# An encoder layer with 32 experts on one core: transposes moved to VectorE, expert matrices loaded in 16 KB runs

## The reference

```python
u2 = modulate(rmsnorm(x, norm_ffn_g[l]), sh_ffn, sc_ffn)     # h * (1 + scale) + shift
# route: sigmoid(u2 @ w_router), best of 8 groups, then top 2 of its 4 experts
def expert_block(args):
    xblk, e = args
    h = jax.nn.silu(xblk @ w_gate[e]) * (xblk @ w_up[e])       # 1024 -> 512
    return h @ w_down[e]                                       # 512 -> 1024
x = x + gt_ffn * (sum over a token's two experts of weight * expert output)
return rmsnorm(x, final_g)
```

## Time and profile before

| | |
|---|---|
| median of three runs | 1627.49 us (1622.82 to 1628.82) |
| the profiled execution | 1622.71 us, its span 1620.9 us |
| mean granted TensorE clock | 0.962 of full speed |
| busy share of the span | PE 92%, PEld 65%, DVE 50%, ACT 27%, POOL 33% |
| DMA | 345.05 MB in 167551 packets, mean 213 GB/s |
| chain that ended last | PE 77%, DMA 11%, DVE 7%, rest 5% |

### The profile page before, as it was taken

The page is one execution under the profiler, slowest core; times in us unless marked ns, Lnnn a source line. Parts: engine busy times, 40 slices in busy tenths (PEclk is TensorE's granted clock), DMA queues, the critical chain, the costliest instruction groups (busy, mean ns, idle before and its releaser), DMA issues.

```text
span 1620.9 us, 32501 instructions
## 1 busy us (share of the span) xinstructions
PE 1486.0 (92%) x12727; PEld 1052.6 (65%) x12727; DVE 815.1 (50%) x1192; ACT 437.4 (27%) x812; POOL 534.7 (33%) x458
## 2 busy tenths in 40 slices
PE   4899999999999999999998998499699798989994
PEld 3677787777778887787886886355355454545551
DVE  4655544555673324445223744455365544645556
ACT  5455553344461112002002321111111111111113
POOL 2532224333344323323231110244243333424453
PEclk9899999999999999999999998699899999989998
DMA  9570113222214333342121612999999999999997
GB/s 340 150 241 29 31 31 96 69 76 66 62 34 143 115 111 91 118 161 75 49 91 38 213 78 108 405 405 403 408 403 404 403 407 405 403 406 359 402 405 283
DMA packets 167551, 345.05 MB, mean 213 GB/s; under 512 B 28073, under 2 KB 96353, under 8 KB 159281
## 3 DMA queue, kind: packets, MB, share of 16 engines
q1 hardware_dynamic: 138544, 288.72, 47.7%
q0 software_dynamic: 19680, 37.65, 6.7%
q10 hardware_dynamic: 9248, 17.58, 3.5%
HBM read 311.41 MB, written 32.39 MB: 212 GB/s over the span
## 4 chain that ended last, share of the span: by engine, by line
PE 77%; DMA 11%; DVE 7%; ACT 2%; issue 2%; SPq 1%; POOL 1%; ACTq 0%; DVEq 0%; POOLq 0%
PE ps L822 30%; PE ps L1094 15%; DMA w_exp<-in_w_exp_up 8%; PE ps L991 7%; PE ps L1104 7%; PE ps L1015 4%; PE ps L886 2%; PE ps L859 2%; PE ps L1077 2%; PE ps L912 1%; PE ps L950 1%; PE ps L961 1%; PE ps L1084 1%; PE ps L873 1%; DVE br_lo L1608 1%
## 5 line engine op out<-in xcount | busy, mean ns | idle before, releaser
L1094 PE MATMUL ps<-w_exp,xT 128*32 128x256 f32 x4992 | 295.3, 390 | 40.5 <-DMA w_exp<-in_w_exp_up 34.6
L822 PE MATMUL ps<-u_hi,w_hi 128*128 128x512 f32 x768 | 308.5, 402 | 6.8 <-DVE u_lo L1513 6.6
L822 PE MATMUL ps<-u_hi,w_lo 128*128 128x512 f32 x768 | 300.3, 391 | 0.0
L822 PE MATMUL ps<-u_lo,w_hi 128*128 128x512 f32 x768 | 300.0, 391 | 0.0
L1094 PEld LDWEIGHTS ps<-w_exp,xT 128*32 128x32 f32 x4992 | 158.0, 112 | 146.4 <-issue 51.3
L614 POOL CAST w_hi<-w_raw 128x1024 fp32r<-128x1024 f32 x48 | 62.5, 1301 | 382.9 <-PE ps L822 232.7
L1852 DVE COPY w_down<-w_exp 128x4096 f32<-128x4096 f32 x78 | 179.7, 2304 | 0.0
L822 PEld LDWEIGHTS ps<-u_hi,w_hi 128*128 128x128 f32 x768 | 144.9, 189 | 45.3 <-issue 9.7
L822 PEld LDWEIGHTS ps<-u_hi,w_lo 128*128 128x128 f32 x768 | 144.7, 188 | 31.1
L822 PEld LDWEIGHTS ps<-u_lo,w_hi 128*128 128x128 f32 x768 | 145.1, 189 | 29.3 <-issue 1.0
L1104 PE MATMUL ps<-w_down,actT 128*32 128x256 f32 x2496 | 150.9, 382 | 2.7 <-DVE w_down L1852 2.7
(11 more groups left out here) (282 smaller groups left out, 2131.3 us busy)
## 6 DMA issues: line engine op xcount, KB each, us to landing
w_exp<-in_w_exp_gate SPq DMA_DIRECT2D x32, 2048.0 KB, 26.6
w_exp<-in_w_exp_up SPq DMA_DIRECT2D x32, 2048.0 KB, 29.3
w_exp<-in_w_exp_down SPq DMA_DIRECT2D x32, 2048.0 KB, 28.7
ada_g<-in_ada_w ACTq DMA_DIRECT2D x32, 512.0 KB, 3.7
w_raw<-in_w_in SPq DMA_DIRECT2D x24, 512.0 KB, 4.1
w_raw<-in_w_branch_gate SPq DMA_DIRECT2D x24, 512.0 KB, 4.0
d_y<-yb POOLq DMA_DIRECT2D x78, 128.0 KB, 8.6
bias<-d_table SPq DMA_DIRECT2D x48, 192.0 KB
```

What stands on the lines that cost most here:

```text
L822: ins = pe.matmul(ps[:, 5 + h, :], a[par][:, kc, :], b[:, kc, HF[h]], start=(n == 1), stop=(n == MM))
L1094: last = pe.matmul(ps[CAP * n:CAP * (n + 1), 2, 0:QT], x, w[n // 2][:, off:off + QT], start=(kc == 0), stop=(kc == KC - 1))
```

## The change

The transposes inside the expert stage go from TensorE to VectorE, whose `transpose` turns each 32x32 block of a tile in its place. Four things follow from it.

- **Rows.** `row_features` turns `xg_s` straight to `xT`, without PSUM; it waits for the copied rows (`xg_s_ready`) and for the end of the `gate_up` that still reads `xT` (`gu_ps`). `next_rows` of ScalarE waits for `xT_ready` in place of TensorE's transposes. `rows_to_features` and the PSUM bank are gone.
- **Hidden values.** `hidden` multiplies in two halves of 64x128 into a new tile `act_q` of 128x128, which `hidden_features` turns to `actT`. `hidden_to_features` is gone. `gate_up` of the next block waits until both halves are done (`act_ready`), as they read its PSUM bank. VectorE's order becomes `row_features` of p+1, `hidden`, `output_of_last_block`, `hidden_features`, `down_weights`.
- **Orders.** A block-wise turn leaves the features of a token in another order than a whole transpose. So the features of u2 are written in a new order ("place" order): VectorE reads x1, `sc_row`, `sh_row` and `sh_b` with a step of eight floats where it makes u2 and the shift row; `normed_features` then transposes contiguous slices. `gate_up` reads the matrices' columns (its moving operand) with a step of four floats, 16 bytes, where it read runs of 256; the router's rows are laid out to match: SyncE loads them with eight DMAs of 128-byte pieces into `wr_rows`, and GpSimd regroups them by three copies that stand behind its `m_lo` of the second tile and wait for `ld_wr`.
- **Runs.** As the order of features is free now, each partition takes one run of 16 KB of each expert matrix.

The core of the diff:

```diff
@@ -202,15 +202,17 @@
 wr = at("wr", 202, [P, KC, NE])
+wr_rows = at("wr_rows", 203, [P, KC, NE])
...
 xg = [at(f"xg{h}", 192 + h, [P, QT]) for h in range(2)]
-xT = at("xT", 194, [P, 2, P])
+xT = at("xT", 194, [P, KC * CAP])
 xg_s = at("xg_s", 195, [P, QT])
...
 y_s = at("y_s", 197, [P, QT])
-actT = at("actT", 198, [P, 2, 2 * CAP])
+actT = at("actT", 198, [P, FC * CAP])
+act_q = at("act_q", 198.5, [P, FC * CAP])
 yb = [at(f"yb{h}", 199 + h, [P, QT]) for h in range(2)]
@@ -362,10 +364,12 @@
 wo_v = w_out[0].rearrange("(c p) n -> p c n", p=P)
-wr_v = w_router.rearrange("(p c) n -> p c n", c=KC)
-exp_v = {"g": w_exp_gate[0].rearrange("e (q p c) n -> e p q (c n)", q=4, p=P),
-         "u": w_exp_up[0].rearrange("e (q p c) n -> e p q (c n)", q=4, p=P),
-         "d": w_exp_down[0].rearrange("e (h p c) n -> e p h (c n)", h=2, p=P)}
+wr_v = w_router.rearrange("(q f h j) n -> h j f q n", q=4, h=2, j=FC)
+exp_v = {"g": w_exp_gate[0].rearrange("e (p c) n -> e p (c n)", p=P),
+         "u": w_exp_up[0].rearrange("e (p c) n -> e p (c n)", p=P),
+         "d": w_exp_down[0].rearrange("e (p c) n -> e p (c n)", p=P)}
+by_place = lambda a: a.rearrange("p (q j f) -> p q j f", q=4, j=KC)
+by_feature = lambda a: a.rearrange("p (q f j) -> p q j f", q=4, j=KC)
 u2_rows = d_u2.rearrange("t (q n) -> (t q) n", q=4)
@@ -534,13 +538,13 @@
                 sp.dma_start(dst[:], src.partition_broadcast(P)).then_inc(ld_rows, 16)
-    wr_g, wr_vg = wr[:].rearrange("p c (g e) -> p c g e", e=EPG), wr_v.rearrange("p c (g e) -> p c g e", e=EPG)
-    for g in range(NG):
-        sp.dma_start(wr_g[:, :, g, :], wr_vg[:, :, group_at(g), :]).then_inc(ld_wr, 16)
+    for h in range(2):
+        for j in range(FC):
+            sp.dma_start(wr_rows[CAP * j:CAP * (j + 1), h::2, :], wr_v[h, j]).then_inc(ld_wr, 16)
     def load_expert(i, w):
         r, _ = matrix_at(i, w)
-        sp.dma_start(w_exp[r][:].rearrange("p (q n) -> p q n", q=2 if w == "d" else 4), exp_v[w][expert_at(i)]).then_inc(ld_wt[r], 16)
+        sp.dma_start(w_exp[r][:], exp_v[w][expert_at(i)]).then_inc(ld_wt[r], 16)
@@ -702,6 +706,12 @@
         pool.tensor_tensor(m_lo[t % 2][:], merged[:, :, t * P:(t + 1) * P], m_hi[t % 2][:].bitcast(f32), SUB).then_inc(m_ready, 1)
+        if t == 1:
+            pool.wait_ge(ld_wr, 16 * 2 * FC)
+            by_group = lambda a: a.rearrange("p c (g e) -> p c g e", e=EPG)
+            for a in range(3):
+                own = slice(3 * a, min(3 * a + 3, NG))
+                pool.tensor_copy(by_group(wr[:])[:, :, own, :], by_group(wr_rows[:])[:, :, a::3, :]).then_inc(wr_ready, 1)
@@ -772,7 +782,7 @@
 def _(pe):
-    for s_, n_ in ((pr_ps, PR_PRIME), (acc_ps, 1), (gu_ps, 1), (y_ps, 1), (y_evac, 2), (yb_ready, 4), (wd_ready, 1), (actT_ready, 1), (xg_s_ready, 1)):
+    for s_, n_ in ((pr_ps, PR_PRIME), (acc_ps, 1), (gu_ps, 1), (y_ps, 1), (y_evac, 2), (yb_ready, 4), (wd_ready, 1), (actT_ready, 1), (xg_s_ready, 1), (act_ready, 2)):
         pe.sem_inc(s_, n_)
     def mod_vector(v):
@@ -1019,7 +1029,7 @@
         if t == 0:
-            pe.wait_ge(ld_wr, 16 * NG)
+            pe.wait_ge(wr_ready, 3)
         for kc in range(KC):
@@ -1027,9 +1037,8 @@
     def normed_features(t):
         pe.wait_ge(u2_ready, t + 1)
-        v = u2[:, t, :].rearrange("p (q c) -> p c q", c=KC)
         for kc in range(KC):
-            last = pe.transpose(ps[:, 4 + kc // 4, (kc % 4) * P:(kc % 4 + 1) * P], v[:, kc, :], ident[:])
+            last = pe.transpose(ps[:, 4 + kc // 4, (kc % 4) * P:(kc % 4 + 1) * P], u2[:, t, kc * P:(kc + 1) * P], ident[:])
         last.then_inc(x2t_ps, 1)
@@ -1070,46 +1079,30 @@
-    def rows_to_features():
-        v = xg_s[:].rearrange("p (m c) -> p c m", c=2)
-        for c in range(2):
-            last = pe.transpose(ps[:, 0, c * P:(c + 1) * P], v[:, c, :], ident[:])
-        last.then_inc(xg_ps, 1)
-    def hidden_to_features():
-        v = act[2 * CAP:P, :].rearrange("p (m c) -> p c m", c=2)
-        for c in range(2):
-            last = pe.transpose(ps[:, 4, c * 2 * CAP:(c + 1) * 2 * CAP], v[:, c, :], ident[2 * CAP:P, 2 * CAP:P])
-        last.then_inc(ht_ps, 1)
     def gate_up(i):
...
         for kc in range(KC):
-            x = xT[:, kc % 2, CAP * (kc // 2):CAP * (kc // 2 + 1)]
             for n in range(4):
-                off = kc * FE + QT * (n % 2)
-                last = pe.matmul(ps[CAP * n:CAP * (n + 1), 2, 0:QT], x, w[n // 2][:, off:off + QT],
-                                 start=(kc == 0), stop=(kc == KC - 1))
+                cols = w[n // 2][:, kc * FE:(kc + 1) * FE].rearrange("p (c a f j) -> p a c j f", c=2, a=2, j=FC)
+                last = pe.matmul(ps[CAP * n:CAP * (n + 1), 2, 0:QT].rearrange("p (c j f) -> p c j f", c=2, j=FC),
+                                 xT[:, CAP * kc:CAP * (kc + 1)], cols[:, n % 2], start=(kc == 0), stop=(kc == KC - 1))
         last.then_inc(gu_ps, 1)
     def down():
         for fc in range(FC):
-            a = actT[:, fc % 2, CAP * (fc // 2):CAP * (fc // 2 + 1)]
+            a = actT[:, CAP * fc:CAP * (fc + 1)]
             for n in range(4):
...
-    def gate_up_and_next_rows(i, p):
+    def gate_up_of_block(i, p):
         pe.wait_ge(xT_ready, p)
+        pe.wait_ge(act_ready, p * 2)
+        hold(pe)
         gate_up(i)
-        pe.wait_ge(xg_s_ready, p + 2)
-        hold(pe)
-        rows_to_features()
     def down_of_last_block(p):
@@ -1117,26 +1110,17 @@
-    def hidden_rows(p):
-        pe.wait_ge(act_ready, p)
-        hold(pe)
-        hidden_to_features()
     read_ends(12)
-    pe.wait_ge(xg_s_ready, 2)
-    rows_to_features()
     for i in range(NE):
...
         if i == 0:
-            gate_up_and_next_rows(0, 1)
-            hidden_rows(1)
+            gate_up_of_block(0, 1)
         read_ends(1)
         with pe.Fori(ends[i - 1] if i else 2, ends[i]) as p:
-            gate_up_and_next_rows(i, p)
+            gate_up_of_block(i, p)
             down_of_last_block(p)
-            hidden_rows(p)
     down_of_last_block(ends[NE - 1])
@@ -1394,7 +1378,7 @@
         if free is not None:
-            sc.wait_ge(xg_ps, free)
+            sc.wait_ge(xT_ready, free)
         hold(sc)
@@ -1680,9 +1664,11 @@
     dve.wait_ge(ld_rows, 16 * 5)
-    ch.mark(dve.tensor_tensor(sh_row[:], sh_row[:], sh_b[:], ADD))
     ch(dve.tensor_tensor(sc_row[:], sc_row[:], sc_b[:], ADD))
     ch(dve.scalar_tensor_tensor(sc_row[:], sc_row[:], 1.0, g_row[:], ADD, MUL))
+    sh_turned = g_row
+    ch(dve.tensor_tensor(by_place(sh_turned[:]), by_feature(sh_row[:]), by_feature(sh_b[:]), ADD))
     def mix_half(t, h):
@@ -1694,7 +1680,7 @@
         ch(dve.reciprocal(ms2[:, m:m + 1], rstd2[:, m:m + 1]))
-        dve.scalar_tensor_tensor(u2[:, m, :], u2[:, m, :], ms2[:, m:m + 1], sh_row[:], MUL, ADD).then_inc(u2_ready, 1)
+        dve.scalar_tensor_tensor(u2[:, m, :], u2[:, m, :], ms2[:, m:m + 1], sh_turned[:], MUL, ADD).then_inc(u2_ready, 1)
     def lower_features(m):
@@ -1709,7 +1695,7 @@
             lower_features(t - 1)
-        ch(dve.tensor_tensor(u2[:, t, :], x1[:, t, :], sc_row[:], MUL))
+        ch(dve.tensor_tensor(by_place(u2[:, t, :]), by_feature(x1[:, t, :]), by_feature(sc_row[:]), MUL))
     normed(TT - 1)
@@ -1827,12 +1813,20 @@
     def row_features(p):
-        dve.wait_ge(xg_ps, p)
-        dve.tensor_copy(xT[:].rearrange("p a b -> p (a b)"), ps[:, 0, 0:2 * P]).then_inc(xT_ready, 1)
+        dve.wait_ge(xg_s_ready, p + 1)
+        dve.wait_ge(gu_ps, p)
+        hold(dve)
+        dve.transpose(xT[:], xg_s[:]).then_inc(xT_ready, 1)
     def hidden(p):
         dve.wait_ge(silu_ready, p)
-        dve.tensor_tensor(act[2 * CAP:P, :], act[2 * CAP:P, :], ps[2 * CAP:P, 2, 0:QT], MUL).then_inc(act_ready, 1)
+        dve.wait_ge(actT_ready, p)
+        hold(dve)
+        for c in range(2):
+            cols = slice(P * c, P * (c + 1))
+            dve.tensor_tensor(act_q[2 * CAP * c:2 * CAP * (c + 1), :], act[2 * CAP:P, cols], ps[2 * CAP:P, 2, cols], MUL).then_inc(act_ready, 1)
     def output_of_last_block(p):
@@ -1842,8 +1836,11 @@
     def hidden_features(p):
-        dve.wait_ge(ht_ps, p)
-        dve.tensor_copy(actT[:].rearrange("p a b -> p (a b)"), ps[:, 4, 0:4 * CAP]).then_inc(actT_ready, 1)
+        dve.wait_ge(act_ready, p * 2 + 2)
+        dve.wait_ge(y_ps, p)
+        hold(dve)
+        dve.transpose(actT[:], act_q[:]).then_inc(actT_ready, 1)
     def down_weights(i):
@@ -1853,16 +1850,16 @@
     row_features(1)
+    row_features(2)
     hidden(1)
-    row_features(2)
     hidden_features(1)
...
         with dve.Fori(last, end) as p:
+            row_features(p + 1)
             hidden(p)
-            row_features(p + 1)
             output_of_last_block(p)
```

More of the change, by code:

```diff
@@ L336, in build @@
         ld_gmix = sem("ld_gmix")
-        ld_rows, ld_wr = sem("ld_rows"), sem("ld_wr")
+        ld_rows, ld_wr, wr_ready = sem("ld_rows"), sem("ld_wr"), sem("wr_ready")
         mo_ps, x1_half, root2, u2_ready, x2t_ps, u2T_ready, ro_ps = (sem(n) for n in (
@@ L347, in build @@
```

(4 more changed lines are left out.)

## The result

The changed kernel takes 1794.88 us in the median of four runs (1792.34 to 1795.47); the kernel before takes 1625.55 beside it. The ratio is 1.104, with a 95% interval from 1.101 to 1.107: 169 us more, where 12 less were forecast. The profiled execution took 1795.18 us with a span of 1793.2.

A forecast was written before the change was run, and what follows sets the result against it. TensorE's matmuls, broken by waits for expert weights, were taken as the bound. Up to the last wait -12 us, the last 22 blocks -2, outside the blocks +2: -12 on 1627.5 gives 1616 us; 8-in-10 range 1600 to 1700.

The forecast's parts named there:

- The step of the moving operand: gate_up's reading of every fourth float, 16 bytes apart, was taken to add zero to its 3.59 us.
- Rival (3): gate_up slowed by its moving operand's step: 1668 us at 5.6 us, 1790 us if doubled to 7.2; chance 0.30.
- The runs' price for the small packets: Expert stage: stores delayed by 16 KB packets make the loop 6.45 us a block while DMA engines are full.
- 12 us gained in front of the last wait: Expert stage: the last wait for weights ends 12 us earlier, from 16 us less DMA work over 32 experts.
- The landing's value: Stores of yb in the expert stage land after 11.6 us with 16 KB packets, against 8.6 in the median.
- eight turns: A store's packets alternate with weight packets on the DMA engines; eight more waits of 309 ns add 2.5 us.
- Rival (4): Store landing grows wholly with packet size, to 14 us, loop 7.6 us a block: 1650 us; chance 0.10.
- TensorE's 0.82 us a block: Transposes removed from TensorE save 0.44 + 0.38 us a block, 64 us over 78 blocks, if nothing else takes over.
- VectorE's cover: VectorE's work after down, some 3.4 us, fits under the next gate_up's 3.59 us, 0.2 us thin.
- The packets: Expert weight loads: a 16 KB packet takes 628 ns on a DMA engine, against 320 for 8 KB.
- Outside the blocks: VectorE's stepped reads of u2 and sh_row, before the mix and behind its last tile, cost 1 us each: +2 us.
- GpSimd's wait for the router's rows: It stands in front of m_lo of tile 2; bounded at 0 to 2 us, taken as 0.

The follow-up runs named there:

- e2: Kernel before with one edit, the 16-byte step in gate_up's moving operand; 1871.05 us in one run.
- e3: Changed kernel with a step of 8 bytes in place of 16 in gate_up's moving operand; 1635.1 us in one run.
- e4: Changed kernel with a step of 32 bytes in place of 16 in gate_up's moving operand; 1798.54 us in one run.
- e7: Kernel before with one edit, expert matrices in runs of 16 KB, transposes still on TensorE; 1634.3 us in one run.
- e1: Changed kernel with gate_up reading runs of 128 floats, the step moved to VectorE's transpose of act_q; 1637.73 us, ratio to before 1.0062.
- e8: e1 (16 KB runs kept) with a third yb buffer; 1633.38 us, ratio to before 1.0051.
- e9: e8 with a third xg buffer as well; 1623.6 us, ratio to before 0.9993.
- e5: e1 with each expert matrix loaded by two DMAs of 8 KB runs; 1614.5 us, ratio to before 0.9934.
- e10: Kernel before with one edit, gate and up matrices in runs of 8 KB in place of 4; 1616.55 us, ratio 0.9953.
- e12: Kernel before with 64 unused matmuls ahead of the mix's last half tile, half with a 16-byte step in the moving operand; 1660.1 us.

## Why the prediction was wrong

**The step of the moving operand** was the term that failed. It was taken at zero, "the weakest choice", because the weight loads cost the same at 8 as at 32 bytes and their 0.5 ns a column is less than the 0.88 that gate_up has. It costs 7.25 - 3.59 = 3.66 us a block, 0.89 ns a column (16 records of 256 columns in each column group): as much again as a column has. The weight loads were the nearest row by name, but their price did not carry over; VectorE's reduce, with its factor of 1.7, came nearer to the 2.0 measured. Rival (3), at its doubled end, gave 7.2 us for gate_up, a block of 9.06 and 1790 us (1792 by its own sum, 1627.5 + 165): measured 7.25, 9.00 and 1794.88. It had 0.30, and the range was cut at 1700 in the middle of it. The rule of the Trainium skill that the prediction named beside it (SBUF — State Buffer, Door 1) spoke for the rival, without a size, and e2, e3 and e4 agree with it in all three sizes. The same passage, though, lets fp32 be read with a step of up to four elements for free; a step of four is what this kernel takes, and measured it is not free.

**The runs' price for the small packets** is the second miss, 23 us wide and hidden behind the first. The sum had 12 us gained in front of the last wait; e7 shows a loss of about 11 from the runs alone. The landing's value was close (11.6 us forecast, 11.8 in the changed kernel with the engines 84% busy, 13.3 in e1 with full ones), but the form was wrong: it counted eight turns of the store and left out the gathers in the same queue (a block's small packets are 12 on each engine), and it made a loop of the landing, which in e8 and e9 grew with each buffer. The two landings that gave the eight turns were also less pure than it says: beside the first ran 545 pieces of 4 KB and 73 of 8 KB, beside the second 303 and 250. Rival (4) had the direction.

**TensorE's 0.82 us a block** came, and more: 1.09 in e5. That the stage would not profit, as stores or loads decide, was right.

**VectorE's cover** held: turns of 445 and 302 ns (0.42 and 0.3 to 0.4 forecast), and the copy of w_down ends 0.27 us ahead of down in e5 (1257.65 to 1257.92), 0.2 forecast.

**The packets**: 113.97 MB in 90.9% of 16 x 300 us in e9 are 26.1 bytes per ns, 627 ns for 16 KB; 628 were forecast. In e5 8 KB take 321.

**Outside the blocks**: the groups of VectorE's lines show the step's price there, in the changed kernel:

```profile
L1698 DVE TENSOR_TENSOR u<-x,sc_row 128x1024 f32<-128x1024 f32 x8 | 17.5, 2186 | 0.0
...
L1671 DVE TENSOR_TENSOR g_row<-sh_row,sh_b 128x1024 f32<-128x1024 f32 x1 | 2.1, 2136 | 0.0
```

Both took 1.22 us before, so about 1 us more each, as forecast. The multiply-add behind it rose from 1.29 to 1.54, which was not. The first gate_up came 3.6 us later; in other kernels it moved by as much without any change there (1038.9 in e7, 1045.1 in e10), so the +2 is seen in the rows only. GpSimd's wait for the router's rows lasted 12.1 us and ended before the next m_hi was there: no cost, as taken.

## What to carry to other kernels

Give a matmul's moving operand at least two of the elements that it reads in each 16 bytes; if a layout has to be turned, put the step on an operand of an engine that has time (here VectorE's transpose of act_q: 0.41 us in place of 0.30, beside 3.45 us of gate_up). Before a bulk transfer is given longer runs, count the small packets that share its engines: where the queues take turns, a block's small packets on one engine times the length of a bulk packet is about what the block takes while the bulk queue is full. Here runs of 8 KB won 7 to 9 us (e10, e5) where 16 KB lost 10. A term of a sum that no row prices is the one to bound widely: its dearest end belongs in the range.

## What the runs showed of the hardware

- A matmul whose moving operand has a step of 16 bytes runs at half rate, for a single stream (e12: 234 to 460 ns for 512 columns in fp32r, 219 to 452 ns a record of 256 in fp32) as for the four groups of gate_up (3.59 to 7.25 us); with 32 bytes gate_up takes 7.39 us, with 8 bytes 3.63. Weight loads are another matter: 206 and 198 ns at 8 and 32 bytes, 140 in a run.
- VectorE turns 128x256 floats by 32x32 blocks in 445 ns, about as long as its copy of that tile took (425 ns, L1831 before).
- GpSimd's gather instruction took 3.10 us where it began beside VectorE's copy of w_down (1306.58, in the first fence of the result) and 0.99 in the kernel before, where it began ahead of the copy (1187.77, the copy at 1188.57). It ended 0.87 us after the copy, so it stood still while the copy ran. The Trainium skill (SBUF — State Buffer, SBUF: two separate sides) says that GpSimd can't write descriptors while such a copy of VectorE runs; the trace agrees. Here it was hidden.
- A DMA engine with two queues waiting takes one packet from each in turn: in e9 a packet of the small queue is followed by one of the other in 97 of 100 cases, and the reverse in 97; with 4 and 8 KB packets the former holds in over 90 (before, e5). With 16 KB packets on the one, a deeper buffer on the other lengthened the landing (13.3, 17.4 and 20.6 us for stores in e1, e8 and e9).
